# Hybrid encoder step: a ring of seven slots, tokens scaled once into DRAM, constants on another queue, and the pieces of the front placed anew

## The chip, the cores and the metric

The kernel runs on one core of one Trainium2 chip. The metric is the time of one execution on the device in microseconds (us). The kernel before takes 3700.74 us, the median of three runs (3699.85 to 3709.32).

## What is computed

A step of one layer for 1152 tokens of width 1024, all in 32-bit floats: 1024 tokens of a prompt and 128 tokens of eight running streams. After the two norms and the mixer comes PEER, a retrieval that fetches 128 rows per token from a table:

```python
h = _rmsnorm(xp, norm_mix[l])
qr, kr, vr, gr, qa, ka, va = _in_proj(h, w_in[l], pos_p)       # z = h @ w_in
xp = xp + _merge(retention, gr, attention, w_out[l], xp.dtype)
xp = xp + _peer(_rmsnorm(xp, norm_ffn[l]), ...)
...
q = (h @ w_q).reshape(T, PEER_HEADS, 2, PEER_DKH)
s = jnp.einsum('tpsd,psnd->tpsn', q, keys)                      # 16 score rows of 128 keys
eidx = the 16 best of the 256 best pairs, for each of 8 heads    # 128 experts per token
act = jax.nn.gelu(jnp.einsum('td,tpkd->tpk', h, u_tab[eidx]))
return jnp.einsum('tpk,tpkd->td', gate * act, v_tab[eidx])
```

## The kernel before, in words

The tokens are nine tiles of 128 (one per partition): tile 0 holds the eight streams (the "sample"), tiles 1 to 8 the prompt. For each tile the program has a **front** (mixer, then router) that ends in the numbers of 128 experts and their gates, and then 128 **choices**. Choice n of the whole program (n from 0 to 1151) is: POOL gathers for each token one row of `uv` (u and v of its expert side by side, 8 KB) into slot n % RING of `ring` (L528, 1 MB per gather); DVE multiplies the u half by h and sums it to a weight (L1346); ACT applies gelu and the gate (L1025, L1027); then v times weight is added to the tile's sum, either on DVE into `y2` (L1379) or on PE with a diagonal matrix that ACT makes (L1033, L894). `on_dve` (L208) says which; `LAG` puts DVE's addition two choices later. POOL may refill a slot when the choice that used it RING earlier has been added (L522 to L527).

The order on every engine is written by hand: `run` (L230) walks over numbered steps. At a step from `G0` on it emits one choice, and each thread (a Python generator) emits its next piece when the step that it yielded comes up. Steps before `G0` carry only the threads. `AT_SAMPLE` gives the steps of the front of tile 0, all before `G0`; `AT_PROMPT` those of the front of tile j, counted from the first choice of tile j-1, so that a front runs beside the choices of the tile ahead of it. Every engine works through its own list in order; a waiting instruction holds back all behind it.

The input projection z = norm(x) @ w_in runs as 54 **groups** (`Z_GROUPS`, L181): a tile by a slice of 512 columns of w_in (256 for slice 5), eight matmuls on PE (L687), an evacuation by ACT (L937), a store of z to DRAM by SP (L566). Groups 0 to 5 are tile 0, 6 to 11 tile 1, 12 to 53 run slice by slice over tiles 2 to 8. `Z_SLOTS` (L183) sets their steps: 26 lie ahead of `G0`, 28 behind it, one every three choices. A group reads the transposed tokens from one of two slots (`hT_slots`): SP loads them (`tokens`, L551), and POOL multiplies them by the norm's weight there (`gains`, L487, L492), once per group from group 12 on. w_in slices go through two slots too (`slices`, L541). All other loads are on SP's queue as well (`constants`, L568), among them eight for the streams' state (L585). SP also stores the streams' new keys and values (16 small stores, L612 and L614).

## Time and profile before

| | us |
|---|---|
| median of three runs | 3700.74 |
| the profiled execution | 3721.22 |
| its span, first to last instruction | 3719.5 |
| first gather issued | 350.67 |
| PE, DVE, ACT, POOL busy | 2883.9, 2304.8, 1277.7, 1414.8 |
| mean granted TensorE clock | 0.92 of 2.4 GHz |

The profile is one execution seen by the hardware profiler. The span is cut into stages by the first gather (350.67) and by the 128th, which is issued just ahead of 900 us. A timeline row gives the start, the time from start to end, engine, line, operation, output and inputs, how many instructions are merged into it, and in brackets how long the engine was idle before it and what ended that. Each 32-bit matmul shows as two records, so that a group is 16 records. SPq is a DMA issue on SP's queue, and its time is that of issuing.

### The profile page before, as it was taken

The numbers are of one execution on the slowest core, as the hardware profiler recorded it, in microseconds if no ns is written. First come the engines' busy times: TensorE is split into PE (matmuls) and PEld (weight loads), VectorE is DVE, ScalarE is ACT, GpSimd is POOL, SyncE is SP. The second block draws the span as 40 slices with busy tenths as digits, with TensorE's granted clock in tenths as the row PEclk, the third lists the DMA queues.
The fourth block names the chain that finished last, engine by engine and source line by source line (L and its number), as shares of the span: only waits on it lengthen the run. The fifth ranks groups of instructions, "written<-read, shape, count | busy, mean of one in ns | idle before, by whom it ended". The sixth has DMA issues, their size and how long they took to land. (4 is left out here: it accounts for less than half of the span.)

```text
span 3719.5 us, 30065 instructions
## 1 busy us (share of the span) xinstructions
PE 2883.9 (78%) x9022; PEld 1443.6 (39%) x9022; DVE 2304.8 (62%) x5212; ACT 1277.7 (34%) x3781; POOL 1414.8 (38%) x1215
## 2 busy tenths in 40 slices
PE   6998667526888788788877887888788778977776
PEld 2654233422444245334523452344245334522222
DVE  0213655686667657766775676567667766775555
ACT  2111211113433443434344433433343434343333
POOL 1012333333344444434443444344334334434443
PEclk9899788758999999999999999999999999999998
DMA  7645777889999999999999999999999999999998
GB/s 249 252 147 176 283 275 273 317 346 415 370 386 405 406 366 395 414 394 372 387 399 395 384 394 402 380 368 397 405 362 401 411 407 362 407 381 415 410 411 345
DMA packets 238229, 1344.83 MB, mean 362 GB/s; under 512 B 30944, under 2 KB 54112, under 8 KB 89312
## 3 DMA queue, kind: packets, MB, share of 16 engines
q0 software_dynamic: 165888, 1208.03, 81.2%
q1 hardware_dynamic: 72176, 134.86, 10.2%
q8 instruction: 71, 1.16, 0.1%
q14 instruction: 94, 0.77, 0.1%
HBM read 1325.11 MB, written 18.61 MB: 361 GB/s over the span
## 5 line engine op out<-in xcount | busy, mean ns | idle before, releaser
L894 PE MATMUL psum<-ring_sb,diag_sb 128*128 128x512 f32 x3696 | 1896.9, 648 | 604.0 <-ACT diag_sb L1033 603.1
L1346 DVE SCALAR_TENSOR_TENSOR ring_sb<-ring_sb,h_sb 128x1024 f32<-128x1024 f32 x1152 | 1416.1, 1230 | 1035.1 <-DMA ring_sb<-uv,expert_sb 1023.7
L528 POOL DMA_INDIRECT ring_sb<-uv,expert_sb x1152 | 1308.4, 1136 | 1754.7 <-PE psum L894 1127.0
L894 PEld LDWEIGHTS psum<-ring_sb,diag_sb 128*128 128x128 f32 x3696 | 683.8, 201 | 1600.4 <-ACT diag_sb L1033 972.6
L1025 ACT ACTIVATE weight_sb<-weight_sb 128x1 f32<-128x1 f32 x1152 | 232.5, 202 | 1890.3 <-DVE ring_sb L1346 1889.6
L687 PE MATMUL psum<-pool_sb 128*128 128x512 f32 (+1 forms) x864 | 381.7, 596 | 58.7 <-DMA pool_sb<-w_in 22.9
L1033 ACT ACTIVATE diag_sb<-ident_sb,weight_sb 128x128 f32<-128x128 f32 x924 | 370.9, 401 | 67.9 <-PE psum L894 38.2
L1027 ACT ACTIVATE weight_sb<-weight_sb,gate_sb 128x1 f32<-128x1 f32 x1152 | 339.2, 294 | 37.4
L869 PEld LDWEIGHTS psum<-front_sb,pool_sb 128*128 128x128 f32 x2304 | 296.4, 195 | 114.8 <-issue 98.7
L869 PE MATMUL psum<-front_sb,pool_sb 128*128 128x128 f32 x2304 | 297.9, 279 | 19.3 <-DMA pool_sb<-w_q 16.1
L1379 DVE SCALAR_TENSOR_TENSOR y_sb<-ring_sb,weight_sb,y_sb 128x1024 f32<-128x1024 f32 x219 | 298.4, 1363 | 1.4 <-ACT weight_sb L1027 1.4
L492 POOL TENSOR_TENSOR pool_sb<-pool_sb,gainT_sb 128x1024 f32<-128x1024 f32 x44 | 96.8, 2201 | 525.6 <-DMA pool_sb<-xT 511.4
L687 PEld LDWEIGHTS psum<-pool_sb 128*128 128x128 f32 x864 | 174.0, 208 | 238.2 <-issue 206.5
L825 PE MATMUL psum<-w_out_sb,front_sb 128*128 128x512 f32 x288 | 127.7, 599 | 3.5 <-ACT front_sb L972 3.5
L1346 DVE DVE_READ_ACCUMULATOR ring_sb<-ring_sb,h_sb 128x1 f32 x1152 | 94.5, 82 | 0.0
L1055 DVE COPY held_sb<-held_sb 128x1 f32<-128x1 f32 x270 | 40.2, 149 | 73.6 <-ACT front_sb L992 72.5
L843 PE MATMUL psum<-keys_sb,front_sb 128*128 128x128 f32 x288 | 42.2, 294 | 55.8 <-ACT front_sb L1003 55.8
L825 PEld LDWEIGHTS psum<-w_out_sb,front_sb 128*128 128x128 f32 x288 | 55.2, 192 | 73.9 <-issue 68.3
L843 PEld LDWEIGHTS psum<-keys_sb,front_sb 128*128 128x128 f32 x288 | 39.2, 208 | 61.2 <-ACT front_sb L1003 56.8
L937 ACT ACTIVATE pool_sb<-psum,x_rstd_sb 128x512 f32<-128x512 f32 (+1 forms) x48 | 30.9, 643 | 88.6 <-PE psum L687 61.0
L1237 DVE FIND_INDEX8 front_sb<-front_sb 128x8 uint32<-128x128 f32 (+1 forms) x216 | 56.7, 262 | 0.0
L1238 DVE MATCH_REPLACE8 front_sb<-front_sb 128x128 f32<-128x128 f32 (+1 forms) x216 | 54.6, 253 | 0.0
(154 smaller groups left out, 1434.7 us busy)
## 6 DMA issues: line engine op xcount, KB each, us to landing
pool_sb<-w_in SPq DMA_DIRECT2D x15, 2048.0 KB, 10.3
pool_sb<-xT SPq DMA_DIRECT2D x44, 512.0 KB, 7.5
ring_sb<-uv,expert_sb POOLq DMA_INDIRECT x1152, 9.5
pool_sb<-w_q SPq DMA_DIRECT2D x16, 1024.0 KB, 8.7
front_sb<-z SPq DMA_DIRECT2D x8, 1408.0 KB, 10.4
z<-pool_sb SPq DMA_DIRECT2D x40, 256.0 KB, 4.8
pool_sb<-w_q SPq DMA_DIRECT2D x4, 2048.0 KB, 58.0
x_sb<-x SPq DMA_DIRECT2D x9, 512.0 KB, 7.2
```

Of the source, the lines that this page charges most:

```text
L492: eng.tensor_tensor(hT_slots[u % 2], hT_slots[u % 2], spread(gainT[:, :], 2, P), ALU.mult)\
L528: eng.indirect_dma_start(out=uv[n % RING], out_offset=None, in_=dr["uv"], in_offset=bass.IndirectOffsetOnAxis(ap=expert[:, j % 2, k:k + 1] ...
L687: mm = eng.matmul(bank(g % 4)[:, 0:w], hT_slots[u % 2][:, k, :], rows[:, k, :], start=(k == 0), stop=(k == KC - 1))
L825: mm = eng.matmul(bank(6 + n), catT[:, k, :], w_out[:, k, n * BANK:(n + 1) * BANK], start=(k == 0), stop=(k == KC - 1))
L843: mm = eng.matmul(bank(4 + g % 2)[:, i * P:(i + 1) * P], rqT[:, g % 2, i, :], keys[:, SLICE * g + i, :], start=True, stop=True)
L869: mm = eng.matmul(out, rows, hT[:, k, :], start=(k == 0), stop=(k == KC - 1))
L894: mm = eng.matmul(bank(b + half), diag[d % DIAGS][:, :], uv[n % RING][:, D + half * BANK:D + (half + 1) * BANK], start=first, stop=last)
L1025: eng.activation(weight[:, one], weight[:, one], ACT.Gelu_apprx_tanh).then_inc(gl_ready, 1)
L1027: eng.activation(weight[:, one], weight[:, one], ACT.Copy, scale=gate[:, j % 2, one]).then_inc(weight_ready, 1)
L1033: eng.activation(diag[d % DIAGS][:, :], ident[:, :], ACT.Copy, scale=weight[:, one])\
L1346: eng.scalar_tensor_tensor(out=u, in0=u, scalar=1.0, in1=h[:, j % 2, :], op0=ALU.mult, op1=ALU.mult, accum_out=weight[:, k:k + 1]).then_in ...
L1379: eng.scalar_tensor_tensor(out=y2[:, :], in0=uv[n % RING][:, D:2 * D], scalar=weight[:, k:k + 1], in1=(x if first else y2)[:, :], op0=ALU. ...
```

## The change

- `RING` is 7 instead of 6. The room comes from `y2` and one of two slots of `h`: the sums now go to `y`, and the router writes its h into `front` (`h_front`), while DVE computes h again at a tile's first choice (`h_kept`).
- The tokens of tiles 2 to 8 are scaled once: SP loads each transposed tile into `x` or `gain_final` (idle then), POOL multiplies it (L528 of the new file), SP stores it to a new DRAM tensor `hTm`. The 42 groups from 12 on load `hTm` and need no POOL work.
- Most constants, the streams' state among them, are issued from ACT's queue. The norm weights and first tokens come ahead of w_in on SP's.
- `G0` is 214. The two halves of a group have steps of their own. 14 groups lie ahead of `G0` and 40 behind. The fronts' steps are new. Four slices of w_q for tile 0 go into free parts of `ring`, so six of eight can be loaded early. The two expansions of the selected numbers have a buffer each (`repeated`).
- In tile 0, DVE adds 124 choices instead of 100, one choice later instead of two; in tiles 1 to 7 14 instead of 16, right behind the choice's own dot product (`late_sum`); in tile 8 one instead of 16.

```diff
-RING = 6
+RING = 7
-G0 = 112
+G0 = 214
 AT_PROMPT = dict(
-    load=0, rope=(3, 4, 5, 6), rota=7, qkT=8, qkT_copy=(9, 10), qTd=11, sc=11, scT=12, sw1=12, sw0=13,
...
+    load=0, rope=(3, 4, 5, 6), rota=7, qkT=8, qkT_copy=(10, 11), sc=11, sw1=12, scT=13, sw0=13, qTd=14,
...
-Z_SLOTS = ((2, 5, 8, 11, 13, 15) + (18, 26, 28, 31, 37, 40) + (62, 65, 70, 73, 79, 82, 86, 90, 94, 97, 100, 103, 106, 109)
-           + tuple(G0 + 3 * i for i in range(28)))
+Z_SLOTS = (((8, 11), (15, 18), (22, 25), (29, 31), (33, 36), (40, 43))
+           + ((48, 69), (70, 138), (140, 142), (180, 182), (184, 187), (190, 193))
+           + ((197, 200), (204, 208))
+           + tuple((G0 + 3 * i, G0 + 3 * i + 1) for i in range(40)))
 def on_dve(n):
-        return k < 100
+        return k < 124
     if j == TILES - 1:
-        return k % 8 == 6
-    return 38 <= k < 44 or (50 <= k < 84 and k % 4 == 2) or k == 90
+        return k == 30
+    return 42 <= k < 48 or (56 <= k < 90 and k % 4 == 2)
 
 gains():    # on POOL
-                for u in range(len(Z_LAST_OF_X)):
-                    first_g = min(g for g in range(len(Z_GROUPS)) if z_x_of(g) == u)
-                    yield 0 if u < 2 else Z_SLOTS[first_g] - 3
-                    eng.wait_ge(xT_loaded[u % 2], 16 * (u // 2 + 1))
+                for u in range(2):
+                    yield 0
+                    eng.wait_ge(xT_loaded[u], 16)
...
+                for i in range(TILES - 2):
+                    yield 30
+                    eng.wait_ge(xT_in[i % 2], 16 * (i // 2 + 1))
+                    eng.tensor_tensor(scaled[i % 2], scaled[i % 2], spread(gainT[:, :], 2, P), ALU.mult)\
+                       .then_inc(xT_scaled, 1)
 
 tokens():    # on SP
+                for u in range(2, len(Z_LAST_OF_X)):
+                    g = Z_FIRST_OF_X[u]
+                    i = Z_GROUPS[g][2] - 2
+                    yield max(Z_SLOTS[g][0] - 8, Z_SLOTS[Z_LAST_OF_X[u - 2]][1] + 1)
+                    eng.wait_ge(z_psum, Z_LAST_OF_X[u - 2] + 1)
+                    eng.wait_ge(hTm_stored[i % 2], 16 * (i // 2 + 1))
+                    eng.dma_start(hT_slots[u % 2], dr["hTm"][i]).then_inc(xT_loaded[u % 2], 16)
+            def scale_tokens():
+                for i in range(TILES - 2):
+                    yield 30 + 5 * i
+                    if i >= 2:
+                        eng.wait_ge(hTm_stored[i % 2], 16 * (i // 2))
+                    eng.dma_start(scaled[i % 2], dr["xT"][ORDER[i + 2]]).then_inc(xT_in[i % 2], 16)
+                    if i:
+                        store_scaled(i - 1)
...
+            def store_scaled(i):
+                eng.wait_ge(xT_scaled, i + 1)
+                eng.dma_start(dr["hTm"][i], scaled[i % 2]).then_inc(hTm_stored[i % 2], 16)
 
 constants():    # now on ACT
+                yield 0
+                eng.dma_start(mode[:, :], dr["mode_tab"][1]).then_inc(mode_loaded, 16)
...
+                yield 36
+                eng.wait_ge(zeroed, 2)
+                for r in range(2):
+                    for q in range(PAIRS):
+                        eng.dma_start(S0[64 * r:64 * r + 64, q, :, 64 * r:64 * r + 64], dr["s0"][r, :, q])\
+                           .then_inc(sample_loaded, 16)
+                yield 51
+                eng.dma_start(w_out[:, :, :], dr["w_out"].rearrange("(k p) n -> p k n", p=P)).then_inc(w_out_loaded, 16)
...
 dot_choice(n):    # on DVE
+                    if k == 0:
+                        if n:
+                            eng.wait_ge(dot_ready, n)
+                        eng.scalar_tensor_tensor(out=h[:, :], in0=x[:, :], scalar=rstd[:, 0:1], in1=gain_ffn[:, :],
+                                                 op0=ALU.mult, op1=ALU.mult).then_inc(h_kept, 1)
...
-                if LAG <= n and n - LAG < STEPS_ALL and on_dve(n - LAG):
-                    add_choice(n - LAG)
+                if 0 < n <= CHOSEN and on_dve(n - 1):
+                    add_choice(n - 1)
+            def late_sum(n):
+                if CHOSEN <= n < STEPS_ALL and on_dve(n):
+                    add_choice(n)
```

Three places show how the instructions move. First PE between the transposes of the mixer's output for tile 0 (L813 before, L860 now) and the router's queries (L869, L917); L687 and L726 are groups of the input projection, L825 and L872 the output projection, L833 and L880 the transposes of h. Before:

```order
L813 MATMUL psum<-ident_sb,front_sb 128x128 x8
L687 MATMUL psum<-pool_sb 128x512 x8
L825 MATMUL psum<-w_out_sb,front_sb 128x512 x3
L687 MATMUL psum<-pool_sb 128x512 x4
L825 MATMUL psum<-w_out_sb,front_sb 128x512 x3
L687 MATMUL psum<-pool_sb 128x512 x4
L825 MATMUL psum<-w_out_sb,front_sb 128x512 x10
L687 MATMUL psum<-pool_sb 128x512 x12
L833 MATMUL psum<-ident_sb,h_sb 128x128 x8
L687 MATMUL psum<-pool_sb 128x512 x4
L869 MATMUL psum<-front_sb,pool_sb 128x128 x32
L687 MATMUL psum<-pool_sb 128x512 x4
```

and now:

```order
L860 MATMUL psum<-ident_sb,front_sb 128x128 x8
L872 MATMUL psum<-w_out_sb,front_sb 128x512 x16
L726 MATMUL psum<-pool_sb 128x512 x12
L880 MATMUL psum<-ident_sb,front_sb 128x128 x8
L917 MATMUL psum<-front_sb,pool_sb 128x128 x32
L917 MATMUL psum<-front_sb,ring_sb 128x128 x8
L890 MATMUL psum<-keys_sb,front_sb 128x128 x4
```

The groups between and behind these pieces are gone from this stretch but for one and a half; eight matmuls are one group.

Second SP's queue around the 16 small stores of the streams' new keys and values (L612, L614 before; L631, L633 now, in pairs). Before, these issues led up to the first pair:

```order
L585 DMA ring_sb<-s 64x8x64 x8
L587 DMA ring_sb<-vc 128x8x128
L548 DMA pool_sb<-w_in 128x8x512 x2
L612 DMA o_ks<-front_sb 16x128
L614 DMA o_vs<-front_sb 16x128
```

and now these follow from the last pair on:

```order
L631 DMA o_ks<-front_sb 16x128
L633 DMA o_vs<-front_sb 16x128
L565 DMA pool_sb<-w_in 128x8x512
L587 DMA x_sb<-xT 128x1024
L595 DMA hTm<-gain_final_sb 128x1024
L565 DMA pool_sb<-w_in 128x8x512
```

The seventh load of w_in (the second of the pair `x2` on L548 before, for group 6) stood ahead of the stores and stands behind them now, as L565.

Third POOL from its last setup to the first choices. Before (one multiplication L492 and three gathers L528 alternate, 26 times in all):

```order
L511 IOTA starts_sb 128x8
L492 TENSOR_TENSOR pool_sb<-pool_sb,gainT_sb 128x1024 x16
L528 DMA ring_sb<-uv,expert_sb 128x2048
L492 TENSOR_TENSOR pool_sb<-pool_sb,gainT_sb 128x1024
L528 DMA ring_sb<-uv,expert_sb 128x2048 x3
L492 TENSOR_TENSOR pool_sb<-pool_sb,gainT_sb 128x1024
```

and now (L528 is the scaling of the last three tiles, L545 the gather):

```order
L528 TENSOR_TENSOR x_sb<-x_sb,gainT_sb 128x1024
L528 TENSOR_TENSOR gain_final_sb<-gain_final_sb,gainT_sb 128x1024
L528 TENSOR_TENSOR x_sb<-x_sb,gainT_sb 128x1024
L545 DMA ring_sb<-uv,expert_sb 128x2048 x1152
L248 UNCONDITIONAL_BRANCH
```

No multiplication is left among the gathers.

## Rows read from the trace of the kernel before

**Rows 1.** The page's DMA queues: packets, MB, share of 16 engines' span.

```profile
q0 software_dynamic: 165888, 1208.03, 81.2%
q1 hardware_dynamic: 72176, 134.86, 10.2%
```

**Rows 2.** Windows by stage: busy us of each engine (instructions), granted clock, DMA share, GB/s.

```profile
0.00:350.67 350.67, 294.37 (x1181) 179.30 (x1182) 83.09 (x317) 60.60 (x96) 44.20 (x37) 0.93 0.59 197
350.67:800.00 449.33, 270.83 (x912) 160.01 (x910) 272.75 (x433) 80.85 (x247) 169.11 (x118) 0.79 0.79 293
800.00:900.00 100.00, 39.92 (x72) 15.43 (x72) 77.16 (x194) 28.83 (x87) 30.76 (x33) 0.69 1.02 409
...
1252.00:1604.00 352.00, 290.26 (x918) 143.81 (x916) 241.03 (x572) 141.39 (x424) 148.12 (x129) 0.95 0.97 393
```

**Rows 3.** Windows of 20 us in the opening.

```profile
40.00:60.00 20.00, 13.46 (x35) 6.98 (x34) 5.02 (x10) 6.46 (x13) 0.00 (x0) 0.83 1.08 331
```

**Rows 4.** Timeline of PE, up to the first gather.

```profile
17.76 15.93 PE L687 MATMUL psum<-pool_sb 128*128 128x512 f32 x32 [17.76 <-POOL pool_sb L492]
...
72.46 9.04 PE L687 MATMUL psum<-pool_sb 128*128 128x512 f32 x16 [11.32 <-DMA pool_sb<-w_in]
...
89.82 1.71 PE L716 MATMUL psum<-front_sb 64*128 64x128 f32 x16
...
146.47 1.95 PE L777 MATMUL psum<-ring_sb 128*128 128x128 f32 x16
...
213.25 8.75 PE L825 MATMUL psum<-w_out_sb,front_sb 128*128 128x512 f32 x20
...
236.44 7.31 PE L869 MATMUL psum<-front_sb,pool_sb 128*128 128x128 f32 x64
...
309.83 48.54 PE L687 MATMUL psum<-pool_sb 128*128 128x512 f32 x112
```

**Rows 5.** Timeline of SP's queue in the opening.

```profile
45.35 15.67 SPq L585 DMA_DIRECT2D ring_sb<-s  x8
...
85.13 0.37 SPq L612 DMA_DIRECT2D o_ks<-front_sb  x1
...
92.49 1.06 SPq L548 DMA_DIRECT2D pool_sb<-w_in  x2
```

**Rows 6.** Line L548, the loads of w_in: from issue to landing.

```profile
DMA to landing us min/median/max: 6.8/9.9/15.7
```

**Rows 7.** Timeline of ACT: the copies of the transposed attention weights, tile 0.

```profile
127.87 1.93 ACT L964 COPY front_sb<-psum 128x1024 f32<-128x1024 f32 x2
```

**Rows 8.** Timeline of DVE, up to the first gather.

```profile
107.31 1.22 DVE L1123 SCALAR_TENSOR_TENSOR front_sb<-psum,tab_sb 128x1024 f32<-128x1024 f32 x1 [5.22 <-PE psum L737]
...
192.62 0.76 DVE L1211 TENSOR_TENSOR front_sb<-psum,rden_sb 128x256 f32<-128x256 f32 x2
...
226.18 1.28 DVE L1263 SCALAR_TENSOR_TENSOR h_sb<-x_sb,rstd_sb,gain_ffn_sb 128x1024 f32<-128x1024 f32 x1
...
310.70 0.15 DVE L1055 COPY held_sb<-held_sb 128x1 f32<-128x1 f32 x1 [18.76 <-ACT front_sb L992]
```

**Rows 9.** Timeline of DVE, the gates of tile 0.

```profile
345.56 0.29 DVE L1336 TENSOR_TENSOR gate_sb<-front_sb,esum_sb 128x128 f32<-128x128 f32 x1
```

**Rows 10.** Timeline of POOL among the choices of tile 0.

```profile
610.51 2.71 POOL L492 TENSOR_TENSOR pool_sb<-pool_sb,gainT_sb 128x1024 f32<-128x1024 f32 x1 [9.86 <-DMA pool_sb<-xT]
...
626.14 2.76 POOL L492 TENSOR_TENSOR pool_sb<-pool_sb,gainT_sb 128x1024 f32<-128x1024 f32 x1 [9.30 <-DMA pool_sb<-xT]
```

**Rows 11.** All waits: engine, line, releaser, us in total, times, longest.

```profile
POOL pool_sb L492 <- DMA pool_sb<-xT: 511.4, 38, 121.0
```

**Rows 12.** Windows of 22 us in the choices of tile 2 (1252 to 1604 us).

```profile
1340.00:1362.00 22.00, 21.75 (x84) 12.22 (x83) 6.85 (x13) 7.39 (x21) 11.02 (x9) 0.94 0.83 319
```

**Rows 13.** Timeline of PE, the same eight transposes in tiles 0 and 1.

```profile
193.43 1.09 PE L813 MATMUL psum<-ident_sb,front_sb 128*128 128x128 f32 x8 [1.68 <-DVE front_sb L1211]
...
541.09 1.97 PE L813 MATMUL psum<-ident_sb,front_sb 128*128 128x128 f32 x8 [21.35 <-DVE front_sb L1211]
```

More of the change, by code:

```diff
@@ L227, in pe_adds, with run @@
     return n - DVE_BEFORE[n]
-def run(threads, steps, first, last):
+def run(threads, steps, first, last, after=None):
     due = [next(t, None) for t in threads]
@@ L237, in run @@
                 due[i] = next(t, None)
+        if after and s >= G0:
+            after(s - G0)
     assert not any(d is not None for d in due)
@@ L456, in program @@
         y_stored = sem("y_stored")
-        stat_slots = (y[:, :], y2[:, :], h[:, 0, :], h[:, 1, :])
+        stat_slots = (y[:, :], h[:, :], ring[:, 12288:13312], ring[:, 13312:14336])
+        scaled = [t[:, :].rearrange("p (k t) -> p k t", k=KC) for t in (x, gain_final)]
         def own_blocks(at4, q):
@@ L782, in mixer, with state @@
                 mm.then_inc(o_psum, 1)
+                def state(hh):
+                    q = hh // 2
+                    eng.wait_ge(vm_ready, hh + 1)
+                    if hh >= 2:
+                        eng.wait_ge(S_ready, hh - 1)
+                    eng.matmul(bank(5 + hh % 2), kd[:, q * P:(q + 1) * P],
+                               vm[hh % 2].rearrange("p b e -> p (b e)"), start=True, stop=True).then_inc(st_psum, 1)
+                if sample:
+                    yield at(j, "st")
+                    eng.wait_ge(pT_ready, 2)
+                    state(0)
                 for hh in range(HEADS):
@@ L845, in scores @@
                     mm.then_inc(s_psum, 1)
-                per = (AT_PROMPT if j else AT_SAMPLE)["q_per"]
                 for g in range(SLICES):
@@ L852, in router @@
                         for half in range(2):
-                            yield at(j, "q") + (2 * side + half) * per // 2 if j else at(j, "q") + side
+                            yield at(j, "q") + 2 * side + half
                             if side == 0 and half == 0:
@@ L875, in router @@
                             scores(g - 1)
-                yield at(j, "q") + (SIDES * per + 1 if j else SIDES)
+                yield at(j, "q") + 2 * SIDES + 1
                 scores(SLICES - 1)
@@ L1012, in router @@
                 eng.wait_ge(rank_ready, j + 1)
[L1013 to L1014 removed]
+                eng.copy(repeated[1], spread(rank, 2, TOPK)).then_inc(repeated_ready, 1)
             def weigh_choice(n):
@@ L1208, in mixer @@
                 steps.wait()
+                if sample:
+                    state(HEADS - 2)
+                    state(HEADS - 1)
                 eng.wait_ge(oa_psum, j + 1)
@@ L1310, in router @@
                 eng.tensor_tensor(rank, place, mask, ALU.bitwise_and).then_inc(rank_ready, 1)
+                pick = [[(slot_of(j - 1) if j else 0) + a for a in part] for part in (AT_PROMPT if j else AT_SAMPLE)["pick"]]
                 eq4 = eq.rearrange("p (h k) r -> p h k r", h=PEER_HEADS)
@@ L1433 @@
     "z": (TILES, P, IN_W),
+    "hTm": (TILES - 2, P, KC, P),
 }
```

282 lines of the change are left out of this document (149 added, 133 removed).

## The prediction

> **What bounds the kernel now.** I read the DMA queues first: the 1152 gathers keep the 16 DMA engines busy for 81.2% of the span, 3020 us or 2.62 us each, and all other transfers for 10.2%, 379 us or 2.81 us per MB [rows 1]. With 0.2% for code loading that is 3407 us of 3719.5, so the engines idle for 312 us, and this is what a change can win. The windows by stage tell where [rows 2]. Up to the first gather the DMA share is 0.59: 144 us idle in 350.67. Among tile 0's choices it is 0.79 (94 us idle), from 800 to 900 us it is full. From 900 us on a tile takes 352 us at about 0.97; up to the end some 74 us idle are left, spread over eight tiles. So the kernel is bound by DMA except in its opening and in tile 0.
>
> The opening is bound by PE: it is busy for 294.37 of 350.67 us [rows 2], and the timeline shows much of that as groups of the projection that tile 0's front does not need. Seven of them take 48.54 us, 6.93 each [rows 4].
>
> Tile 0's choices are bound by a loop through POOL. A multiplication stands ahead of every three gathers; POOL waits 9 to 10 us for its tokens and only then multiplies. One round takes 626.14 - 610.51 = 15.6 us [rows 10], where three gathers need 7.9 us of DMA. POOL waited 511.4 us for such tokens in all [rows 11].
>
> **The sum** goes by three stages: to the first gather (350.67 before), tile 0's 128 choices (to 900, so 549), the rest (2819.5).
>
> **Stage 1, the opening.** Twelve groups leave it, 83 us of PE. What it can shrink to is the chain of tile 0's front, walked piece by piece:
>
> - Group 5 ends at 81.5. PE began at 17.76 and waited 11.32 for the last slice of w_in [rows 4], for SP sat 15.67 us in the eight state loads [rows 5]. These are now on ACT, where nothing due is behind them, and the tokens come first. Bounds: 58 (start at 12, five groups, a half one, one landing in the open) and 81 (nothing gained, as DMA ran full there, share 1.08 [rows 3]). I take 65, near the work of the loads due by then.
> - Here the order turns against the change. The load for group 6 now stands behind the 16 small stores, which wait for group 5's evacuation, and PE's half of group 6 stands ahead of the scores. Evacuation 2, stores 92.49 - 85.13 = 7.4 [rows 5], landing 9.9 [rows 6], half a group 3.5: scores at 88, not at 65 + 8. Scores and window scores take 107.31 - 89.82 = 17.5 [rows 4, 8]: 105.5.
> - From there to the copy of the attention weights 127.87 - 107.31 = 20.6 [rows 7, 8], with two evacuations ahead of the exponentials. One is left. Bounds 8 and 20.6; I take 12, then outputs start at 117.5 (before: 146.47 [rows 4], with four groups more in between).
> - Outputs and states of the heads, 146.47 to 193.4: 47 us [rows 4, 8], partly at low clock. The masked values are now ready ahead of the loop and no piece else is cut: 36 to 47, I take 41: 158.5.
> - Transposes and copy 2; output projection 32 records at 8.75/20 = 0.44 [rows 4], 14; to the end of h 227.5 - 222.0 = 5.5 [rows 4, 8], beside which PE runs one and a half groups (10.4, so 5 more); transposes and copy 2: queries at 187.
> - Queries: 64 records in 7.31 [rows 4], 256 in 29.2; scores 3; half a group 3.6; copies 2: 225. Their w_q slices are loaded early.
> - Last scores to gates 345.56 - 310.70 = 34.9 [rows 8, 9]. ACT no longer has three groups ahead of its first expansion, and the second has its own buffer: 28 to 35, I take 29: 254, first gather at **255** (bounds 240 to 290).
>
> **Stage 2, tile 0.** Work moves here. DMA work was 0.79 x 449.33 + 1.02 x 100 = 457 us [rows 2]; twelve groups bring 12 token loads and 12 stores (9.4 MB) and one slice of w_in (2.1 MB): 32 us at 2.81, 489 in all. Preparing `hTm` costs 14 transfers of 0.52 MB, 21 us of DMA work in the opening, which has 350.67 x 0.41 us of room and keeps 255 - (207 - 32 + 21) = 59. POOL's loop is gone: the group's token load is issued some nine choices ahead and holds up PE, not the gathers. What is late next is PE with ACT: 40 groups of 6.93 are 277 us, the front's other pieces some 100, at the clock of 0.79 [rows 2] 477 us; ACT waits for a group's evacuation ahead of the next weights. DVE has 128 dot products and 124 additions, some 350 us, and its mixer pieces; it hides. Bounds: 500 (489 at share 0.98) and 600 (share 0.81, as now). PE and DMA are nearly equally loaded, so I take share 0.93: **526**.
>
> **Stage 3, the rest.** The idle there comes once per tile, when PE and ACT turn to the mixer: share 0.83 at 1340 to 1362 us with PE busy for 21.75 of 22 [rows 12]. A seventh slot lets one more gather (2.62 us) be on its way. PE gets two additions more per tile (4 us), DVE one more h (1.3), both hidden behind 352 us while PE is busy for 290 [rows 2]. Bounds: 0 to -45. I take about half the idle that returns per tile, 4 us in eight tiles: **2787**.
>
> 255 + 526 + 2787 = 3568, which is 151.5 less than the span 3719.5. The profiled execution (3721.22) lies 20 above the median of the runs shown, so I subtract from that median: 3700.74 - 151.5, about **3549**.
>
> *Two rules against the sum.* In the DMA share of 1.08 from 40 to 60 us [rows 3] a queue was held but the engines were full. The Trainium skill, "DMA: Bandwidth & Descriptors", section "Issuing engines are not separate DMA queues", says that DMAs issued from several engines share the same 16 DMA engines and save only issue time; the trace agrees for that window, and by this rule alone the 16 us at group 5 would be nil and the sum 3565.
>
> **The rivals.**
>
> *A, ring and new steps bring nothing in stage 3.* For it: the engines are already at 0.97, and the wait is PE's own pace. Then 255 + 526 + 2820: **3582**.
>
> *B, tile 0 keeps its pace.* The round of 15.6 us would then not be POOL's but that of ACT, PE and SP: 40 rounds are 624, the last eight choices 21. Against it: what ends POOL's wait is the token load, which leaves its list. 255 + 645 + 2787: **3668**.
>
> *C, PE at the lower clock in tile 0, the slower side.* PE waits there for DVE and ACT pieces, and after such waits it runs slower: eight transposes took 1.97 us after 21.35 us idle, 1.09 in the busy opening [rows 13]. If all of tile 0 ran at that lower level (1.2 GHz), a group takes 6.93 x 1.97/1.09 = 12.5 and the rest 181: 500 + 181 = 681, and with token waits and half a landing per slice some 720, and the total **3743**. It is slower than before once tile 0 takes over 678. Against it: 0.79 of full clock with 28 groups, and more groups keep PE busier. The Trainium skill, "TensorE: Matmul & The Clock Gate", section "HAM oscillation — how this bites in real kernels", says that bursts of matmuls with waits between them fall back to half rate each time; the trace agrees in these two rows.
>
> *D, the opening does not shrink as walked*: the stores ahead of group 6's load and the scaling chain on SP cost 50 us more, first gather at 305: **3599**.
>
> **How the numbers follow.** A difference of 0.3% (11 us) is about what a measurement can tell from none. My forecast has 0.62; A 0.13, B 0.10, C 0.06, D 0.09. All but C are faster by more than that; I leave 0.02 for the gap between B and C. So faster 0.92, same 0.02, slower 0.06. The forecast's own bounds give 3549 - 15 - 26 - 12 = 3496 at the low end and, with the upper bounds of two terms added, about 3640. From 3496 to 3640 holds the forecast, A, D and a part of B.
>
> **What would show it.** Right: the first gather near 255 us, no multiplication and no token wait on POOL after it, a DMA share over 0.9 to the 128th gather near 780 us, 40 groups among tile 0's choices, a tile of 348 us later. An idle PE of 15 to 25 us ahead of group 6, ended by w_in, would show the misplaced load. Wrong: a DMA share of 0.8 in tile 0 with ACT waiting for PE (B or C; the granted clock tells which), or a first gather beyond 290.

## The result, and the profile after

The change makes the kernel faster: 3453.15 us (median of four runs, 3447.9 to 3455.82) against 3705.03 for the kernel before on the same chip, a ratio of 0.9317 (95% interval 0.9294 to 0.934). The forecast was 3549, the range 3496 to 3640: the direction is right, and the gain is over one and a half times the one forecast. The profiled execution took 3455.48 us, with a span of 3453.7.

Where the 265.8 us between the two spans (3719.5 and 3453.7) come from, cut at the first gather and at the first gather of tile 1. The prediction had put the second cut of the kernel before at 900, with the 128th gather just ahead of it; that gather was issued at 909.90 and the first of tile 1 at 912.63. So its three terms are compared as changes.

| stage | before | after | change | forecast |
|---|---|---|---|---|
| opening, to the first gather | 350.67 | 265.04 | -85.6 | -95.7 |
| tile 0's choices | 561.96 | 492.28 | -69.7 | -23 |
| the rest | 2806.9 | 2696.4 | -110.5 | -32.5 |

The opening is 10 us short of the forecast, tile 0 gained three times as much as forecast, and the rest more than three times. Six later tiles (from the 256th to the 1024th gather) took 331.6 us each, 351.0 before; these six give 116, the stretch behind them 7, and tile 1 gave 12 back. The load of w_q for the later tiles (four parts of 2 MB) was issued among tile 0's choices before; now it is issued with tile 1's first choice. SP's queue, before and after:

```profile
798.37 46.20 SPq L655 DMA_DIRECT2D pool_sb<-w_q  x4
...
756.92 30.41 SPq L691 DMA_DIRECT2D pool_sb<-w_q  x4
```

At the full rate of 421 GB/s shown below, these 8.4 MB are some 20 us (an estimate). So a part of tile 0's gain, and of tile 1's loss, is only this move; no run puts the load back.

The DMA queues of the profile after, which answer to [rows 1]:

```profile
q0 software_dynamic: 165888, 1208.03, 85.0%
q1 hardware_dynamic: 67120, 132.10, 10.5%
q10 hardware_dynamic: 7072, 10.10, 0.9%
```

q10 is new: its 10.10 MB are the loads and copies that ACT issues.

Its windows by stage, columns as in [rows 2]; the last three rows are tiles 1, 2 and 3:

```profile
0.00:265.04 265.04, 204.29 (x986) 136.46 (x987) 79.04 (x318) 48.60 (x81) 26.61 (x29) 0.91 0.72 244
265.04:757.32 492.28, 339.99 (x1107) 185.62 (x1105) 352.92 (x662) 125.68 (x346) 161.80 (x129) 0.86 0.93 370
757.32:1120.44 363.12, 279.98 (x910) 141.77 (x910) 238.04 (x566) 139.84 (x419) 162.44 (x129) 0.91 0.97 396
1120.44:1451.83 331.39, 281.56 (x918) 140.32 (x918) 239.29 (x567) 141.04 (x423) 156.61 (x129) 0.97 1.01 414
1451.83:1783.80 331.97, 282.85 (x918) 140.50 (x918) 239.33 (x568) 141.59 (x426) 157.52 (x128) 0.97 1.01 414
```

What to see: tile 0 runs at a DMA share of 0.93, exactly the share that the prediction chose, and yet 34 us under its 526. A later tile runs at 1.01 and 414 GB/s, where [rows 2] has 0.97 and 393. The share rose by 4%, the rate by 5%, and the tile became 5.5% shorter.

The timeline of PE in the opening after, which answers to [rows 4]:

```profile
14.03 16.09 PE L726 MATMUL psum<-pool_sb 128*128 128x512 f32 x32 [14.03 <-DMA pool_sb<-w_in]
...
70.62 1.04 PE L738 MATMUL psum<-ident_sb,front_sb 128*128 128x128 f32 x8
...
99.36 5.80 PE L726 MATMUL psum<-pool_sb 128*128 128x512 f32 x8 [27.05 <-DMA pool_sb<-w_in]
105.09 1.71 PE L755 MATMUL psum<-front_sb 64*128 64x128 f32 x16
...
171.92 15.67 PE L872 MATMUL psum<-w_out_sb,front_sb 128*128 128x512 f32 x32 [1.10 <-ACT front_sb L1020]
...
199.86 7.41 PE L917 MATMUL psum<-front_sb,pool_sb 128*128 128x128 f32 x64 [1.10 <-ACT front_sb L1030]
```

SP's queue in the same stretch, as [rows 5]; the other 15 stores stand between these two rows:

```profile
72.94 0.36 SPq L631 DMA_DIRECT2D o_ks<-front_sb  x1
...
81.18 0.43 SPq L565 DMA_DIRECT2D pool_sb<-w_in  x1
```

Group 5 ends at 70.6. Then PE waits 27.05 us for the slice of w_in of group 6. That load stands behind the 16 small stores, issued from 72.94 to 81.18. This is the misplaced load that the prediction named (it forecast an idle PE of 15 to 25 us there).

### The profile page after: what moved, and what is told of

It is laid out like the page before. It is cut to its first block, busy times and chain, and to the rows that moved or that the text cites. A ratio compares the mean times of both kernels' runs of the same rounds, so it can differ in the third digit from the quotient of the medians.

```text
span 3453.7 us, 30135 instructions
## 1 busy us (share of the span) xinstructions
PE 2784.1 (81%) x9042; PEld 1399.9 (41%) x9042; DVE 2274.4 (66%) x5216; ACT 1287.6 (37%) x3794; POOL 1426.3 (41%) x1180
## 3 DMA queue, kind: packets, MB, share of 16 engines
q0 software_dynamic: 165888, 1208.03, 85.0%
q10 hardware_dynamic: 7072, 10.10, 0.9%
## 4 chain that ended last, share of the span: by engine, by line
DMA 41%; PE 29%; DVE 11%; ACT 9%; issue 7%; SPq 2%; POOL 0%; ACTq 0%; DVEq 0%
DMA ring_sb<-uv,expert_sb 37%; PE psum L942 16%; PE psum L726 6%; DVE ring_sb L1433 5%; DVE y_sb L1468 4%; DMA pool_sb<-w_in 2%; PE psum L917 2%; ACT diag_sb L1075 2%; ACT weight_sb L1069 1%; DMA pool_sb<-w_q 1%; ACT L1067 1%; ACT weight_sb L1067 1%; ACT front_sb L1005 1%; SPq L691 1%; PE psum L872 1%
## 5 line engine op out<-in xcount | busy, mean ns | idle before, releaser
L942 PE MATMUL psum<-ring_sb,diag_sb 128*128 128x512 f32 x3716 | 1826.8, 625 | 472.3 <-ACT diag_sb L1075 471.6
L545 POOL DMA_INDIRECT ring_sb<-uv,expert_sb x1152 | 1399.7, 1215 | 1903.7 <-PE psum L942 1320.9
L942 PEld LDWEIGHTS psum<-ring_sb,diag_sb 128*128 128x128 f32 x3716 | 667.6, 195 | 1426.0 <-ACT diag_sb L1075 822.9
L726 PE MATMUL psum<-pool_sb 128*128 128x512 f32 (+1 forms) x864 | 376.8, 591 | 142.1 <-issue 88.3
L1468 DVE SCALAR_TENSOR_TENSOR y_sb<-ring_sb,weight_sb,y_sb 128x1024 f32<-128x1024 f32 x214 | 274.6, 1283 | 159.3 <-ACT weight_sb L1069 159.3
L917 PEld LDWEIGHTS psum<-front_sb,pool_sb 128*128 128x128 f32 x2176 | 278.7, 194 | 120.1 <-issue 94.3
L917 PE MATMUL psum<-front_sb,pool_sb 128*128 128x128 f32 x2176 | 282.2, 277 | 27.6 <-DMA pool_sb<-w_q 26.5
L726 PEld LDWEIGHTS psum<-pool_sb 128*128 128x128 f32 x864 | 172.1, 205 | 319.9 <-issue 270.1
L872 PE MATMUL psum<-w_out_sb,front_sb 128*128 128x512 f32 x288 | 128.3, 602 | 7.8 <-ACT front_sb L1020 7.8
L985 ACT ACTIVATE pool_sb<-psum,x_rstd_sb 128x512 f32<-128x512 f32 (+1 forms) x48 | 31.1, 648 | 264.6 <-PE psum L726 249.2
L872 PEld LDWEIGHTS psum<-w_out_sb,front_sb 128*128 128x128 f32 x288 | 54.6, 192 | 80.3 <-issue 65.6
L1316 DVE FIND_INDEX8 front_sb<-front_sb 128x8 uint32<-128x128 f32 (+1 forms) x216 | 57.0, 264 | 0.0
L1329 DVE FIND_INDEX8 front_sb<-front_sb 128x8 uint32<-128x128 f32 (+1 forms) x216 | 52.9, 265 | 0.0
L1164 DVE TENSOR_TENSOR front_sb<-front_sb,tab_sb 128x1024 f32<-128x1024 f32 x9 | 11.0, 1222 | 57.6 <-DMA tab_sb<-tile_tab 38.4
## 6 DMA issues: line engine op xcount, KB each, us to landing
ring_sb<-uv,expert_sb POOLq DMA_INDIRECT x1152, 12.2
pool_sb<-w_q SPq DMA_DIRECT2D x12, 1024.0 KB, 11.5
```

The source lines that it names most:

```text
L545: eng.indirect_dma_start(out=uv[n % RING], out_offset=None, in_=dr["uv"], in_offset=bass.IndirectOffsetOnAxis(ap=expert[:, j % 2, k:k + 1] ...
L726: mm = eng.matmul(bank(g % 4)[:, 0:w], hT_slots[u % 2][:, k, :], rows[:, k, :], start=(k == 0), stop=(k == KC - 1))
L872: mm = eng.matmul(bank(6 + n), catT[:, k, :], w_out[:, k, n * BANK:(n + 1) * BANK], start=(k == 0), stop=(k == KC - 1))
L917: mm = eng.matmul(out, rows, hT[:, k, :], start=(k == 0), stop=(k == KC - 1))
L942: mm = eng.matmul(bank(b + half), diag[d % DIAGS][:, :], uv[n % RING][:, D + half * BANK:D + (half + 1) * BANK], start=first, stop=last)
L1316: eng.max_index(where16[:, g, 0:8], best16[:, g, 0:8], values[:, g, :])
```

## The experiments

Each kernel was timed against the kernel before on the same chip. "Tile" is the mean of tiles 2 to 7, from the 256th to the 1024th gather. The first gather, tile 0 and "tile" come from the one profiled execution, the totals are medians of four. The two can differ: the profiled execution of e5 took 3556.3 us, 14 above its median, which is nearly 2 us per tile. Differences of that size between tile times are not explained here.

| run | median us | ratio to before, 95% interval | first gather | tile 0 | tile |
|---|---|---|---|---|---|
| the changed kernel | 3453.2 | 0.9317 (0.9294 to 0.934) | 265.0 | 492.3 | 331.6 |
| e1, six slots | 3491.4 | 0.9431 (0.9391 to 0.9472) | 264.6 | 494.0 | 337.5 |
| e2, old steps | 3472.1 | 0.9397 (0.9355 to 0.9439) | 263.5 | 467.8 | 337.0 |
| e3, six slots and old steps | 3504.3 | 0.9467 (0.9427 to 0.9507) | 263.7 | 477.2 | 342.8 |
| e4, late additions | 3456.6 | 0.9341 (0.9303 to 0.9379) | 264.2 | 495.4 | 331.8 |
| e5, all three old | 3542.2 | 0.9553 (0.9518 to 0.9588) | 263.9 | 473.9 | 348.4 |
| e9, old steps, late additions | 3456.8 | 0.9323 (0.9284 to 0.9362) | 260.9 | 473.2 | 336.1 |
| e12, five slots | 3650.6 | 0.9841 (0.9796 to 0.9885) | 264.2 | 491.4 | 358.9 |
| e7, POOL scales in tile 0 | 3575.4 | 0.9652 (0.9626 to 0.9679) | 267.0 | 609.6 | 332.0 |
| e6, stores behind w_in | 3430.7 | 0.9263 (0.9238 to 0.9288) | 238.3 | 495.7 | 331.5 |
| e8, old steps in tile 1 only | 3434.0 | 0.9279 (0.9256 to 0.9302) | 263.2 | 470.9 | 331.3 |
| e11, constants on SP | 3448.4 | 0.9294 (0.9253 to 0.9336) | 260.6 | 495.6 | 331.9 |
| e10, e6 and e8 together | 3410.4 | 0.9204 (0.9164 to 0.9243) | 236.3 | 470.4 | 331.9 |

### What gave 20 us per later tile: ring, steps, or DVE's additions (e1 to e5, e9, e12)

The forecast had 4 us per tile here. Three parts of the change touch these tiles, and the first four runs take them back singly and in a pair.

**e1, six slots.** The seventh slot's memory stays set aside.

```diff
-RING = 7
+RING = 6
-        ring = sb("ring", [P, RING * 2 * D])
+        ring = sb("ring", [P, 14336])
```

> The changed kernel (3453 us, 331.6 us per steady tile) with the gathers going round six slots instead of seven; the memory of the seventh stays set aside, everything else as it is. Theory R (the ring gives the 20 us per tile, seven steady tiles and tile 1, 8 x 20 = 160 us at most): a steady tile goes back to 345 to 352 us, POOL waits longer for PE's and DVE's additions, total 3560 to 3610 us. Theory S (the new places of the front's pieces give it): a steady tile stays at 332 to 336, total 3455 to 3485. Theory D (the way DVE adds gives it): as S here.

Measured: 337.5 per tile, total 3491.4. It falls between the theories: 5.9 us of the 19.4, neither all nor nothing.

**e2, old steps.** The steps of `AT_PROMPT` and the choices that DVE adds in tiles 1 to 7 as before.

```diff
-    return 42 <= k < 48 or (56 <= k < 90 and k % 4 == 2)
+    return 38 <= k < 44 or (50 <= k < 84 and k % 4 == 2) or k == 90
-    S=31, gn=(33, 34, 35), gstd=35, ret=(38, 39), cat=40, catT=40, catT_copy=42, y=42, y_per=3, x_load=43, x1=50,
+    S=28, gn=(29, 30, 31), gstd=32, ret=(33, 34), cat=35, catT=36, catT_copy=37, y=38, y_per=3, x_load=40, x1=44,
...
```

> The changed kernel with the steps of the prompt tiles' front and the choices that DVE adds in tiles 1 to 6 put back to where they were in the kernel before; ring of seven kept. Theory R: a steady tile stays at 332 to 337 us, total 3455 to 3495. Theory S: a steady tile goes back to 345 to 352, with slices near 300 GB/s at choices 25 to 35 of a tile as in the kernel before, total 3545 to 3610. Theory D: between, since DVE's choices lie differently but the new way of adding stays: 3455 to 3500.

Measured: 337.0 per tile, so 5.4 lost; theory S's 345 to 352 did not come. The total lost only 19 us, because tile 0 became 24.5 us *shorter*, which no theory had. Of that more at e8.

**e3, both.** The edits of e1 and e2.

> Both together: six slots and the old steps. If ring and steps are worth separate amounts, the loss is the sum of the two single losses within 10 us. If the seventh slot only covers what the steps leave open (or the other way round), the loss is more than the sum: each alone costs little, both together bring the 350 us tile of the kernel before back, total near 3600. Theory D alone: no more than 3520.

Measured: 342.8 per tile. 11.2 lost against 5.9 + 5.4 = 11.3, and in the total 51 against 38 + 19: in these surroundings the two are separate amounts. But 342.8 is still 8 us short of the 351 of the kernel before.

**e4, late additions.** In tiles 1 to 8 DVE adds a choice two dot products later, as before.

```diff
                 if 0 < n <= CHOSEN and on_dve(n - 1):
                     add_choice(n - 1)
+                if CHOSEN + 2 <= n < STEPS_ALL + 2 and on_dve(n - 2):
+                    add_choice(n - 2)
...
             def late_sum(n):
-                if CHOSEN <= n < STEPS_ALL and on_dve(n):
-                    add_choice(n)
+                pass
```

> The changed kernel, but in tiles 1 to 8 DVE adds a choice two dot products later, as the kernel before did, instead of right behind its own dot product at the end of the step. POOL's gather of the slot waits for that addition. Theory D: POOL's wait for DVE additions, 7.8 us in a steady tile, goes back towards the 52.5 us of the kernel before, and a steady tile to 340 to 350 us, total 3520 to 3600. Theories R and S: within 10 us of the changed kernel, 3445 to 3465.

Measured: 331.8 per tile, total 3456.6: with seven slots the later addition costs nothing. So none of the three alone was worth more than 6 us, and the sum of the single losses was 11.5, not 19.4. Either the parts cover for one another, or a fourth thing was missing.

**e5, all three old.** The edits of e1, e2 and e4.

> The changed kernel with six slots, the old steps and DVE's additions two dot products late again, all three together. Six slots and old steps gave 342.8 us per steady tile, 351 is the kernel before's, and the late additions alone cost nothing with seven slots (331.8 against 331.6). Theory J (the three cover for one another: with six slots a slot that comes free two choices later can no longer be made up): 348 to 353 us per steady tile, total 3545 to 3570, and the 20 us per tile are then told in full. Theory X (the last 8 us are something else, such as DVE's order in the front or the two sums in y): 342 to 344 per tile, total 3495 to 3515.

Measured: 348.4 per tile, total 3542.2 (just under the forecast 3545). With six slots and the old steps the late addition costs 348.4 - 342.8 = 5.6 us, with seven slots nothing: theory J. What is left to the 351.0 of the kernel before, 2.6 us, no run explains, and it is hardly more than the spread between executions.

**e9, the seventh slot in the old surroundings.** The edits of e2 and e4, ring of seven. This is the price that the prediction had to name.

> Old steps and late additions, but seven slots: against e5_all_old this is the seventh slot by itself, in the surroundings in which the prediction priced it. e5_all_old took 348.5 us per steady tile, old steps with seven slots 336.9. Theory C (with seven slots a slot that comes free two choices later costs nothing, whatever the steps): 336 to 339 per tile, total 3468 to 3490; the slot is then worth 10 to 12 us per tile in the old surroundings and 6 in the new. Theory I (late additions cost their 5.7 us wherever the old steps are): 341 to 344, total 3505 to 3530, and the slot is worth 6 in both.

Measured: 336.1 per tile. So the seventh slot is worth 348.4 - 336.1 = 12.3 us per tile where steps and additions are old, and 5.9 where they are new: theory C in the tile, though the total of 3456.8 lies under its 3468. It is the additions that make the difference: with old steps but new additions (e3 against e2) the slot is worth 342.8 - 337.0 = 5.8, and with seven slots and old steps the late additions cost nothing (336.1 against 337.0 in e2). Tile 3 of e5, as one window:

```profile
1471.64:1819.72 348.08, 286.12 (x910) 140.73 (x910) 241.41 (x569) 140.18 (x421) 143.37 (x129) 0.96 0.98 394
```

What POOL waits for there from DVE (us in total, times, longest):

```profile
POOL ring_sb L545 <- DVE y_sb L1469: 55.1, 16, 5.6
```

The same two of e9:

```profile
1438.93:1775.77 336.84, 283.48 (x911) 139.81 (x910) 240.45 (x568) 139.44 (x421) 146.44 (x129) 0.96 1.00 408
```

and

```profile
POOL ring_sb L545 <- DVE y_sb L1469: 41.1, 15, 4.7
```

POOL still waits for DVE's additions in e9 (41.1 us in 15 waits, 55.1 in 16 in e5). The waits did not go away, and yet the rate rises from 394 to 408 GB/s. The likely reason is that with a seventh slot enough gathers are already on their way when POOL waits; no run shows that step by itself.

**e12, five slots.** As e1, with 5.

> The changed kernel with five slots, everything else new. Six slots cost 6.1 us per steady tile against seven. Theory G (each of two or three stalls per tile empties the ring, and each missing slot is one gather of 2.55 us that is not on its way in it): again 5 to 8 us, 343 to 346 per tile, total 3530 to 3550. Theory H (with five the ring is shorter than the way of one choice, landing of 10 us and 5.7 us until the slot is free against 5 x 2.59 = 13 us): the pace itself falls, 355 to 375 per tile, total 3620 to 3780, with an even, lower rate in all slices.

Measured: 358.9 per tile, total 3650.6. The time is theory H's, but not quite its picture. The rate is low in most of the tile, but not evenly: in 16 equal slices of tile 3 (1514.1 to 1874.8 us) it goes from 317 up to 422 GB/s, with 13 of them at 401 or less and three at 414 or more.

```profile
1581.70:1604.30 22.60, 16.17 (x44) 7.77 (x45) 8.16 (x13) 13.15 (x40) 6.54 (x7) 0.85 0.80 317
...
1852.30:1874.80 22.50, 14.24 (x30) 4.82 (x28) 11.58 (x21) 7.18 (x24) 8.75 (x7) 1.00 1.01 422
```

Neither theory fits whole: G's stalls would have cost 5 to 8 us, and H asked for an even rate. What is measured is that five slots to six bring 21.4 us per tile and six to seven 5.9, while the median gather lands after 8.3, 10.1 and 12.2 us with five, six and seven slots. Each slot added is worth less. That a deeper ring already covers the short waits, so that only the long ones reach DMA, would explain this; it is not shown.

### The opening: the stores ahead of w_in (e6), the queue of the constants (e11)

**e6.** The 16 stores move on SP behind the loads for groups 6 and 7.

```diff
-                        yield at(j, "rota") + 1
+                        yield 47
                         eng.wait_ge(rota_ready, 2)
```

> The changed kernel with the 16 small stores of tile 0's new keys and values moved on SP from step 35 to step 47, behind the loads of w_in for groups 6 and 7. Theory M (the misplaced load of the prediction): the load for group 6 is issued some 15 us sooner, PE's wait of 27.05 us ahead of group 6 falls to 5 to 12, the first gather comes at 245 to 253 instead of 265, total 3433 to 3442. Theory N (the engines are busy with other loads there, so an earlier issue brings no earlier landing): first gather 260 to 267, total 3448 to 3457.

Measured: first gather at 238.3, total 3430.7. Theory M, and more than it forecast. PE's timeline in this run:

```profile
76.13 5.40 PE L726 MATMUL psum<-pool_sb 128*128 128x512 f32 x8 [3.74 <-DMA pool_sb<-w_in]
81.46 1.71 PE L755 MATMUL psum<-front_sb 64*128 64x128 f32 x16
```

SP's queue, the two loads of w_in and the first of the 16 stores:

```profile
62.97 0.38 SPq L565 DMA_DIRECT2D pool_sb<-w_in  x1
...
70.89 0.38 SPq L565 DMA_DIRECT2D pool_sb<-w_in  x1
...
79.82 0.36 SPq L631 DMA_DIRECT2D o_ks<-front_sb  x1
```

The load is issued at 62.97 instead of 81.18, PE waits 3.74 us instead of 27.05, and the scores start at 81.46 instead of 105.09. These 24 us reach the first gather (26.7 sooner) and the total (22 less).

**e11.** The thread `constants` moves from ACT's list to SP's, at the same steps.

```diff
-            run([constants(), token_squares(), fronts(), in_projection()], weigh_choice, 0, G0 + STEPS_ALL + 2 * SUM_AT)
+            run([token_squares(), fronts(), in_projection()], weigh_choice, 0, G0 + STEPS_ALL + 2 * SUM_AT)
...
-            run([tokens(), slices(), statistics(), scale_tokens(), query_slices(), fronts(), z_stores(), y_stores()], lambda n: None,
+            run([constants(), tokens(), slices(), statistics(), scale_tokens(), query_slices(), fronts(), z_stores(), y_stores()], lambda n: None,
```

> The changed kernel with all the loads of constants put back on SP's list at the same steps (mode and sinks first, kcT and vc at 20, the eight state loads at 36, w_out and keys at 51). Theory Q (a queue is held by its own small loads: the eight state loads held SP for 15.67 us before and ACT for 13.09 now, whoever issues them): the loads of w_in stand behind them, PE waits 10 to 17 us more ahead of the groups, first gather 275 to 285, total 3462 to 3475. Theory N (the same 16 engines carry it all, who issues makes no difference beyond the issue itself): first gather 262 to 269, total 3449 to 3459.

Measured: first gather at 260.6, 4 us earlier, and a total of 3448.4 whose interval overlaps the changed kernel's: theory N, both a little under its ranges. SP's queue of this run:

```profile
80.03 5.41 SPq L618 DMA_DIRECT2D ring_sb<-s  x8
85.47 0.62 SPq L565 DMA_DIRECT2D pool_sb<-w_in  x1
...
106.18 0.43 SPq L621 DMA_DIRECT2D w_out_sb<-w_out  x1
```

and PE's wait for group 6 in it:

```profile
94.75 5.99 PE L747 MATMUL psum<-pool_sb 128*128 128x512 f32 x8 [22.69 <-DMA pool_sb<-w_in]
```

The eight state loads take SP 5.41 us here, at a time when the DMA share is 0.63 (80 to 86 us). In the kernel before they took 15.67 [rows 5] at a share of 1.08 [rows 3], and on ACT's queue in the changed kernel 13.09 (issued from 53.13 on, share 1.04). The time that a queue is held by such loads thus went with how full the engines were, not with which queue it is. That moving the constants to ACT's queue won no time of its own (3453.2 with it, 3448.4 without) agrees with the Trainium skill, "DMA: Bandwidth & Descriptors", section "Issuing engines are not separate DMA queues", which the prediction weighed: DMAs share the same 16 DMA engines, whichever engine starts them. But e11 is no full test of theory Q: its state loads stand behind the 16 stores, not ahead of the loads for group 5, and that order with the new steps was not tried.

### Tile 0: POOL's loop (e7) and the steps of tile 1's front (e8)

**e7.** The projection's tokens are loaded unscaled, and POOL multiplies them three steps ahead of their group. The scaling into `hTm` stays.

```diff
+                for u in range(2, len(Z_LAST_OF_X)):
+                    yield Z_SLOTS[Z_FIRST_OF_X[u]][0] - 3
+                    eng.wait_ge(xT_loaded[u % 2], 16 * (u // 2 + 1))
+                    eng.tensor_tensor(hT_slots[u % 2], hT_slots[u % 2], spread(gainT[:, :], 2, P), ALU.mult)\
+                       .then_inc(hTm_ready, 1)
...
-                    eng.dma_start(hT_slots[u % 2], dr["hTm"][i]).then_inc(xT_loaded[u % 2], 16)
+                    eng.dma_start(hT_slots[u % 2], dr["xT"][ORDER[i + 2]]).then_inc(xT_loaded[u % 2], 16)
```

> The changed kernel with the projection's token tiles loaded unscaled again and multiplied by POOL three steps ahead of their group, as the kernel before did, for all 40 groups of tile 0. Theory L (POOL's wait for the tokens ahead of the gathers set tile 0's pace): a round of three choices takes 14.5 to 16 us, tile 0 takes 590 to 650 us instead of 492, total 3550 to 3610. Theory B (PE, ACT and SP set the pace, rival B of the prediction): tile 0 stays at 490 to 525, total 3450 to 3490.

Measured: tile 0 in 609.6 us, total 3575.4: theory L. The loop of [rows 10] is back, with a round of 14.9 us here, and the rate of tile 0 falls from 370 to 298 GB/s. POOL's timeline:

```profile
514.97 2.74 POOL L533 TENSOR_TENSOR pool_sb<-pool_sb,gainT_sb 128x1024 f32<-128x1024 f32 x1 [9.75 <-DMA pool_sb<-xT]
517.86 1.78 POOL L550 DMA_INDIRECT ring_sb<-uv,expert_sb  x1
519.94 0.94 POOL L550 DMA_INDIRECT ring_sb<-uv,expert_sb  x1 [0.30 <-issue]
521.18 0.94 POOL L550 DMA_INDIRECT ring_sb<-uv,expert_sb  x1 [0.30 <-issue]
529.91 1.90 POOL L533 TENSOR_TENSOR pool_sb<-pool_sb,gainT_sb 128x1024 f32<-128x1024 f32 x1 [7.79 <-DMA pool_sb<-xT]
```

Tile 0 of e7 as one window:

```profile
267.00:876.70 609.70, 355.24 (x1106) 196.49 (x1104) 387.33 (x662) 127.18 (x346) 236.01 (x168) 0.79 0.78 298
```

**e8.** The old steps for the front of tile 1 alone, which runs among tile 0's choices; the new ones from tile 2 on.

```diff
-    due = (AT_PROMPT if j else AT_SAMPLE)[what]
+    due = (AT_PROMPT if j > 1 else AT_FIRST if j else AT_SAMPLE)[what]
```

> The changed kernel with the old steps for the front of tile 1 alone, which runs among tile 0's choices, and the new ones from tile 2 on. With the old steps everywhere tile 0 had taken 467.8 us instead of 492.3 and tile 1 370.8 instead of 363.1. If that is the steps' doing in tile 0: tile 0 465 to 472, later tiles 331 to 333, total 3425 to 3438. If it was the other order of DVE's choices in tile 1, or if tile 1 gives it back: tile 0 and 1 together 850 to 856, total 3447 to 3457.

Measured: tile 0 in 470.9, later tiles 331.3, total 3434.0. So the new steps *cost* 21 us in tile 0, where tile 1's front runs, and bring their 5 us per tile only with the fronts of tile 2 and later (tile 1's choices took 370.8 in e2, 363.4 here and 363.1 in the changed kernel). The waits of the changed kernel from 236 to 757 us, which is tile 0's choices and the end of the opening (us in total, times, longest):

```profile
POOL ring_sb L545 <- DVE y_sb L1468: 327.4, 121, 23.1
...
ACT pool_sb L985 <- PE psum L726: 173.4, 20, 25.4
```

The same two of e8, from 236 to 757 us (its tile 0 ends at 734):

```profile
POOL ring_sb L552 <- DVE y_sb L1475: 310.6, 124, 21.5
...
ACT pool_sb L992 <- PE psum L733: 95.3, 16, 23.2
```

Cut at tile 0's own first and last gather, POOL's waits are 328.6 and 307.6 us, and ACT's are unchanged. ACT waited 173.4 us for PE to finish groups, and 95.3 with the old steps: while it waits ahead of a group's evacuation it holds up the weights of the next choices, these DVE's additions, and these POOL's gathers. That this chain carries the 21 us is read from the waits; no run takes it apart.

**e10, both improvements.** The edits of e6 and e8.

> Stores behind the loads of w_in (first gather 238 instead of 265) and the old steps for the front of tile 1 (tile 0 in 471 instead of 492) together. If they are separate: first gather 237 to 240, tile 0 468 to 474, later tiles 331 to 333, total 3402 to 3414. If the earlier start meets the scaled tokens or the loads of w_in in tile 0, one of the gains is lost: tile 0 485 to 500, total 3422 to 3435.

Measured: first gather at 236.3, tile 0 in 470.4, tiles 331.9, total 3410.4, ratio 0.9204 (0.9164 to 0.9243). The gains are separate. It is the fastest version of this study, 43 us under the changed kernel.

## Why the prediction was right or wrong

**Right: the shape of the change.** The opening shrinks as groups leave it (PE's busy time there fell from 294.37 [rows 2] to 204.29; no run puts the groups back), POOL's loop is gone (e7 brings it back for 117 us of tile 0), 40 groups fit among tile 0's choices, and the misplaced load is there. Rival B falls by e7, rival D by the first gather at 265. Rival C did not come: the granted clock of tile 0 is 0.86, above the 0.79 of [rows 2]. That DVE adds 24 choices more in tile 0, and each one choice sooner, was taken back by no run, so its share in tile 0's gain is open.

**The opening, right within 10 us, by pieces that partly cancel.** Forecast and measured: group 5 ends at 65 and 70.6; scores begin at 88 and 105.1; outputs of the heads at 117.5 and 133.9; heads end at 158.5 and about 169; queries at 187 and 199.9; first gather at 255 and 265. After the scores each piece held within 6 us. What failed was the landing of the load for group 6: priced at 9.9 [rows 6], it took about 18 (issued at 81.18, PE went on at 99.36), and the half group behind it took 5.80 us, not 3.5. The trace shows what this load landed among. ACT issued w_out (4 MB), the keys and three smaller transfers from 72.58 on, and from 82 to 100 us the engines were full, at a share of 1.03 (the second row is a window, columns as in [rows 2]):

```profile
72.58 0.39 ACTq L1103 DMA_DIRECT2D w_out_sb<-w_out  x1
...
82.00:100.00 18.00, 0.64 (x1) 0.50 (x2) 0.00 (x0) 0.00 (x0) 0.00 (x0) 0.50 1.03 410
```

In e11 these transfers are issued from 106.18 on, behind the loads of w_in. There the same load was issued 4 us later, at 85.47, and yet PE went on at 94.75, 9.3 us after the issue. This points to the transfers on ACT's queue, behind which the prediction saw nothing due: SP's queue was free of them, the engines were not. e11 moves the other constants as well, so it does not show this alone.

For the 11 us at group 5 the prediction's reason was that the eight state loads leave SP's queue. e11 does not decide this: it has the constants on SP, and group 5 ends at 70.4 too, but its state loads come at 80.03, when the load for group 5 is long issued. Their place, the moved steps and the tokens that come first remain; which of them it was is open.

**The step that failed: DMA work read as share times time.** The prediction took the share as the part of time in which the engines could do no more, so that 0.97 left 9 us of idle time in a tile, of which it gave half to the change, and that 489 us of work waited in tile 0. But it saw 74 us of idle time behind tile 0, and there the change won 110. The share counts the time of packets, and that time is not a fixed amount of work: q0 moved the same 1208.03 MB in 81.2% of 3719.5 us and in 85.0% of 3453.7, which is 2.62 us per gather before and 2.55 after, 85 us less in all. With nothing changed but the ring it is 2.64 with five slots (e12, 83.1% of 3655.6), 2.57 with six (e1, 84.5% of 3499.4) and 2.55 with seven. So a part of the time lost to a short ring is counted as packets at work. Why a packet then takes longer, no run shows. The rate shows the loss. Three windows of 21.8 us in tile 2 of the kernel before (16 from 1263.5 to 1612.7 us):

```profile
1285.30:1307.20 21.90, 15.97 (x44) 6.77 (x45) 18.56 (x31) 11.56 (x31) 9.64 (x8) 1.00 1.01 421
...
1329.00:1350.80 21.80, 16.02 (x43) 7.62 (x42) 7.51 (x14) 12.89 (x39) 6.96 (x6) 0.84 0.81 299
...
1569.10:1590.90 21.80, 16.32 (x32) 6.74 (x31) 14.67 (x20) 8.41 (x25) 9.77 (x8) 0.84 0.88 342
```

Two of the 16 in tile 3 after, a full one and one of the two emptiest:

```profile
1472.60:1493.30 20.70, 14.18 (x29) 5.04 (x30) 16.24 (x28) 10.58 (x29) 7.53 (x8) 0.99 1.01 421
...
1514.10:1534.80 20.70, 16.18 (x36) 7.20 (x35) 11.80 (x22) 13.56 (x43) 8.76 (x8) 0.84 0.97 388
```

The full rate is 421 GB/s, in both kernels. A share of 0.97 goes with 393 GB/s [rows 2], which is 0.93 of it, and 0.79 with 293, which is 0.70. The Trainium skill, "Perfetto Trace Analysis", section "Roofline", puts the bound of the 16 DMA engines at about 435 GB/s when one core is active; the fullest windows of these runs show 421 to 425 (425 in one of e9), and the measurement decides. By the rate a tile before had (1 - 393/421) x 352 = 23 us to win, not 9, and the change won 19.4 of them. In tile 0 the work is 293 x 449.33 + 409 x 100 = 173 MB and 11.5 MB for the twelve groups, 184 MB in all, 437 us at 421 GB/s and not 489. (The prediction left out two things here that nearly cancel: the 5 MB between 900 and 912.63, and the 8.4 MB of w_q that left the stage; measured are 370 x 492.28 = 182 MB, in 0.93 x 492.28 = 458 us of packet time.) With the prediction's own two choices (0.93 of the full rate, and half of a tile's idle time) the three terms would have been 255 + 470 + 2726 = 3451. That this meets the 3453.7 so closely is luck: it is worked out after the result, the half was a guess, and the terms miss one by one. Tile 0 ran at 0.88 of the full rate and took 492, the opening took 265, and the rest won 110 and not 93.

**The price of the seventh slot.** "One more gather (2.62 us) on its way" is the price of one wait that empties the ring, and the prediction counted one such wait per tile; with the new steps and additions, which it held to be hidden, its term came to 4 us per tile where 19.4 were won. Measured the slot alone is 12.3 us per tile in the old surroundings (e5, e9). The windows of the kernel before suggest why once is too few: besides the stretch of [rows 12] there is the one at 1569, with a rate of 342, and seven more of the 16 lie at 375 to 398. That with six slots the many short waits for PE's and DVE's additions reach DMA too is read from these rates, not shown by itself. POOL's waits in that tile before:

```profile
POOL ring_sb L528 <- PE psum L894: 142.6, 85, 8.6
POOL ring_sb L528 <- DVE y_sb L1379: 52.5, 16, 5.2
```

And in tile 3 after:

```profile
POOL ring_sb L545 <- PE psum L942: 162.2, 104, 6.9
POOL ring_sb L545 <- DVE y_sb L1468: 7.8, 5, 1.6
```

POOL waits for about half of the tile in both, and for PE even 20 us longer after, in a tile 17 us shorter. The waits alone do not tell what a slot is worth; the rate does.

**Rival A** (ring and steps bring nothing in the later tiles) was given 0.13 and is refuted: with ring, steps and additions all old (e5) the stretch from the first gather of tile 1 on takes 2816.8 us, 120 more than in the changed kernel.

**The range.** Its upper end, "about 3640", is said to add the upper bounds of two terms; these give 3617, 3655 or 3658, by which two are taken. It does not matter for a result below the lower end, whose sum (3496) is right.

## What to carry to other kernels

Where DMA bounds a stretch, read its idle time from GB/s against the fullest window of the same kernel, not from the busy share, which here hid more than half of what could be won. Compare stretches with like transfers only: in the opening a share of 1.08 went with 331 GB/s [rows 3]. A slot more in a ring of gathers was worth more here than one transfer for the one stall that was seen: price it by all stretches below the full rate, and expect each further slot, and each other repair of the same waits, to be worth less (21.4, 5.9; 12.3 with nothing else repaired). An issue order written by hand should be looked through for small stores that wait ahead of a load that PE needs: 16 of them cost 24 us here (e6) and one number repaired it. And a load moved to another queue still shares the DMA engines: with large constants issued there just ahead, the load that PE needed took 18 us, and 9.3 in e11, where they come later.

## What was not expected

Steps that are better in seven tiles were worse by 21 us in the one whose PE also carries 40 groups (e2, e8): what is the better place of a piece was not the same in every tile. And the same eight loads held their queue for 15.67, 13.09 or 5.41 us, the less the emptier the DMA engines were (shares 1.08, 1.04 and 0.63).
